# A hybrid sliding-window and sparse attention block: value products one head later, search passes dealt by new weights, indexer scores in groups of four, five key slots

## What is computed

```
A: q k^T / 8 - slope * |distance|, window of two 64-token chunks,
   softmax with a learned sink per head, times v        (8 heads, 2 key/value heads)
B: score[t, s] = sum over 4 indexer heads of w[t, h] * relu(q_idx[t, h] . k_idx[s])
   each query keeps the 256 keys of the highest score among those visible to it,
   ties broken by position; softmax over those, times v (8 heads, one shared key/value)
```

## Time and profile before

| | |
|---|---|
| median of 3 runs | 3556.61 us (3550.65 to 3558.83) |
| the profiled execution's own time | 3546.74 us |
| its span | 3545.0 us |
| PE busy | 3068.2 us, 87% of the span |
| DVE busy | 1700.3 us, 48% |
| ACT busy | 1585.2 us, 45% |
| `mixing` in the span | about 105 to 1812 us |

### The profile page before, as it was taken

The page is one execution under the profiler, slowest core; times in us unless marked ns, Lnnn a source line. Parts: engine busy times, 40 slices in busy tenths (PEclk is TensorE's granted clock), DMA queues, the critical chain, the costliest instruction groups (busy, mean ns, idle before and its releaser), DMA issues. The chain is left out here.

```text
span 3545.0 us, 43989 instructions
## 1 busy us (share of the span) xinstructions
PE 3068.2 (87%) x14889; PEld 2499.4 (71%) x14889; DVE 1700.3 (48%) x3080; ACT 1585.2 (45%) x3023; POOL 305.4 (9%) x990
## 2 busy tenths in 40 slices
PE   5788887777887787686889789999999999999997
PEld 2566666665666665666778678788887888788876
DVE  2154556566566765774445444324442444244422
ACT  1356666567656676676443222223222322232222
POOL 0012221111111111111001100000000000000000
PEclk8777878778887888778799999999999999999999
DMA  5011110000000000000035533334333433343323
GB/s 199 21 42 39 32 35 24 18 16 19 25 22 14 14 24 10 4 7 1 5 135 166 170 103 98 91 119 142 95 95 113 142 95 98 111 141 100 95 89 107
DMA packets 316082, 254.94 MB, mean 72 GB/s; under 512 B 9152, under 2 KB 271904, under 8 KB 315808
## 3 DMA queue, kind: packets, MB, share of 16 engines
q1 hardware_dynamic: 282544, 236.29, 21.5%
q10 hardware_dynamic: 33392, 16.81, 1.6%
HBM read 219.50 MB, written 33.57 MB: 71 GB/s over the span
## 5 line engine op out<-in xcount | busy, mean ns | idle before, releaser
L1928 ACT ACTIVATE p_hi<-raw 128x1024 fp32r<-128x1024 f32 x264 | 279.4, 1059 | 695.0 <-PE dbank L1899 356.1
L2002 DVE TENSOR_TENSOR p_lo<-raw,p_hi 128x1024 fp32r<-128x1024 f32 x264 | 323.5, 1225 | 426.9 <-ACT p_hi L1928 426.7
L826 PE MATMUL obank<-vb,probT 128*128 128x64 f32 x2176 | 344.7, 308 | 88.0 <-ACT probT L1084 87.6
L826 PEld LDWEIGHTS obank<-vb,probT 128*128 128x128 f32 x2176 | 333.9, 231 | 98.7 <-ACT probT L1084 98.5
L1084 ACT ACTIVATE probT<-tbank 128x512 f32<-128x512 f32 (+3 forms) x448 | 213.8, 487 | 347.1 <-PE tbank L810 342.8
L1108 ACT ACTIVATE relu<-score,pick 128x512 bf16<-128x512 f32 (+6 forms) x224 | 303.8, 1356 | 48.5 <-POOL pick L603 47.5
L1255 DVE TENSOR_SCALAR_CACHE_REDUCE above<-score,cand 128x384 bf16<-128x384 f32 (+6 forms) x224 | 316.0, 1411 | 4.8
L1880 PE MATMUL gbank<-x_hi,p_hi 128*128 128x512 f32 x704 | 275.5, 391 | 29.4 <-DVE p_lo L2002 29.4
L693 PE MATMUL work<-w_in,h_T 128*128 128x512 f32 (+1 forms) x768 | 298.0, 537 | 0.7 <-ACT h_T L892 0.7
L1897 PE MATMUL dbank<-p_hi,a_hi 128*128 128x512 f32 x704 | 279.0, 396 | 17.0 <-DVE a_lo L2030 14.1
L795 PE MATMUL lbank<-kb,qb_hi 128*128 128x512 f32 (+3 forms) x320 | 170.6, 533 | 138.0 <-DVE mx L1315 92.2
(11 more groups left out here) (219 smaller groups left out, 5314.4 us busy)
## 6 DMA issues: line engine op xcount, KB each, us to landing
raw<-in_w_gate_up SPq DMA_DIRECT2D x176, 512.0 KB, 3.8
raw<-in_w_down SPq DMA_DIRECT2D x88, 512.0 KB, 3.8
ada<-in_w_ada ACTq DMA_DIRECT2D x32, 512.0 KB, 3.8
wada<-in_w_ada SPq DMA_DIRECT2D x4, 2048.0 KB, 15.5
x_in<-in_x SPq DMA_DIRECT2D x16, 512.0 KB, 3.9
mixT<-oT SPq DMA_DIRECT2D x32, 256.0 KB, 2.3
mix<-mixT SPq DMA_DIRECT2D x16, 512.0 KB, 6.2
x_rows<-in_x SPq DMA_DIRECT2D x16, 512.0 KB, 4.4
```

What stands on the lines that cost most here:

```text
L826: mm = nc.tensor.matmul(obank[o % 2][:, h * HD:(h + 1) * HD], probT[:, t % 2, j * P:(j + 1) * P], v, start=(g == 0 and j == 0), stop=(last ...
L1928: nc.scalar.activation(p_hi[:, s], raw[:, s], ACT.Copy).then_inc(panel_high, 1)
L2002: nc.vector.tensor_tensor(p_lo[:, s], raw[:, s], p_hi[:, s].bitcast(F32), ALU.subtract).then_inc(panel_ready, 1)
```

## The change

- **Value products.** `copy_transposed` writes the transposed group back to the bytes of the `logit` row that it came from, and `probT` is gone. `logit` has four rows. All value products of head i-3 are now beside the pieces of head i and the transposes of head i-2; output scaling, turning and copying come a head later each. DVE's first piece of head i waits for `pv_done` of head i-4 in place of `pt_full` of head i-3.
- **Search passes.** `slot_weight` is replaced by one weight function for DVE and one for ACT. Both `ties` actions of a DVE-searched block are in its last slot. On ACT, when more than one sign pass is in a head, one each is put behind the first and the third copy of a transposed group.
- **Scores.** One step per piece of keys, four pairs of products each: the first where the burst was, the next ones after A heads 0, 1 and 2. The projection parts move one head later, the queries of B one head earlier (after A head 2).
- **Keys of A.** `ka` has five slots; a tile whose number is a multiple of four (but the first) is written to slots 0 and 4, so that two neighbouring tiles always lie side by side, and an A head has one pair of products over 256 columns in place of two pairs over 128.
- **Buffers.** `signs` is a tile of its own in int8 and no longer waits for the relus, `above` is uint8 in place of bf16, `bias_v` is gone (`bias_b` serves blocks 0 and 1), and the key/value latent has its own tile `latT_kv`.

```diff
@@ -187,8 +187,29 @@
     return b % 2 == 1
-def slot_weight(kind, b):
-    return 3.0 if kind == "A" else 2.5 + 0.45 * (b + 1)
+def vector_weight(b, slot):
+
+    it, kind, h = slot
+    scoring = it + 2 < NB and h <= 3
+    if kind == "A":
+        return (0.0 if it == b - 2 else 0.5) if scoring else 3.3
+    room = 0.5 + 0.41 * (it + 1)
+    if it + 3 < NB and h in (2, 4, 6):
+        room -= 1.0
+    if it == b - 2 and b > 2:
+        room -= {6: 2.0, 7: 100.0}.get(h, 0.0)
+    return max(room, 0.0)
+
+
+def scalar_weight(b, slot):
+
+    it, kind, h = slot
+    if kind == "A":
+        return 0.0 if it == b - 2 and h <= 3 else 1.8
+    room = 0.5 + 0.3 * (it + 1)
+    if it + 3 < NB:
+        room -= {1: 2.5, 3: 2.5, 5: 2.5, 6: 1.0}.get(h, 0.0)
+    return max(room, 0.3)
@@ -210,16 +231,16 @@
         slots += [(it, "B", h) for h in range(HEADS)]
     vector, scalar = {}, {}
     if searched_by_scalar(b):
-        wts = [slot_weight(kind, it) for it, kind, h in slots[:-2]]
+        wts = [scalar_weight(b, slot) for slot in slots[:-2]]
         for slot, r in zip(slots, spread(wts, len(ON_SCALAR))):
             scalar[slot] = [(b, ON_SCALAR[n]) for n in r]
         vector[slots[-2]] = [(b, AFTER_SCALAR[0])]
         vector[slots[-1]] = [(b, action) for action in AFTER_SCALAR[1:]]
     else:
-        wts = [0.0 if (it, kind, h) == (b - 2, "B", HEADS - 1) else slot_weight(kind, it) for it, kind, h in slots[:-1]]
-        for slot, r in zip(slots, spread(wts, len(SEARCH) - 1)):
+        wts = [vector_weight(b, slot) for slot in slots[:-1]]
+        for slot, r in zip(slots, spread(wts, len(SEARCH) - 2)):
             vector[slot] = [(b, SEARCH[n]) for n in r]
-        vector[slots[-1]] = [(b, SEARCH[-1])]
+        vector[slots[-1]] = [(b, action) for action in SEARCH[-2:]]
     return vector, scalar
@@ -257,8 +278,8 @@
     def front_a(b, h):
-        add(*{0: [("transposes", b)], 2: [("proj", b, 0)], 3: [("proj", b, 1)], 4: [("proj", b, 2)],
-              5: [("proj", b, 3)], 6: [("proj", b, 4)]}.get(h, []))
+        add(*{0: [("transposes", b)], 3: [("proj", b, 0)], 4: [("proj", b, 1)], 5: [("proj", b, 2)],
+              6: [("proj", b, 3)], 7: [("proj", b, 4)]}.get(h, []))
...
@@ -285,7 +306,9 @@
             steps.append(("head", "A", nxt, h, tuple(vector.get(at, ())), tuple(scalar.get(at, ()))))
             if b + 3 < NB:
                 front_a(b + 3, h)
-            if h == 3:
+            if h + 1 < len(key_chunks("B", nxt)):
+                add(("scores", nxt, h + 1))
+            if h == 2:
                 add(("queries", "B", b))
             if h in (1, 7):
@@ -347,6 +370,13 @@
     return [(o, min(BANK, cols - o)) for o in range(0, cols, BANK)]
+def key_slots(t):
+
+    if t == 0 or t % 4:
+        return t % 4, lambda ap: ap
+    return slice(0, 5, 4), lambda ap: ap.unsqueeze(2).to_broadcast([HD, A_KV, 2, P])
+
+
 class Plan:
...
@@ -406,10 +436,9 @@
         neg_half = sb("neg_half", [P, 1])
         ndist = sb("ndist", [P, T], F16)
         bias_a = sb("bias_a", [P, 2 * P])
-        bias_v = sb("bias_v", [P, 2 * P])
         bias_b = sb("bias_b", [P, T])
-        ka = sb("ka", [P, A_KV, 4, P], F32R)
+        ka = sb("ka", [P, A_KV, 5, P], F32R)
         ki = sb("ki", [P, T], F32R)
         kb = sb("kb", [P, T], F32R)
         va = sb("va", [P, 4, P])
@@ -425,13 +454,15 @@
         pj = sb("pj", [P, D_IN])
         kk = sb("kk", [P, 3, 2, HD])
         lat = sb("lat", [P, Q_RANK + KV_RANK])
-        latT = sb("latT", [P, 3, 3, P])
+        latT = sb("latT", [P, 3, 2, P])
+        latT_kv = sb("latT_kv", [P, P])
         widx = sb("widx", [P, 2, IDX_HEADS])
         ssq = sb("ssq", [P, 3])
...
         score = sb("score", [P, 2, T])
-        above = sb("above", [P, T], BF16)
+        above = sb("above", [P, T], mybir.dt.uint8)
+        signs = sb("signs", [P, T], mybir.dt.int8)
         rank = sb("rank", [P, T], F16)
         cand = sb("cand", [P, 1], I32)
...
-                    spans = [(j * P, P, ka[:, g, t % 4, :]) for j, t in enumerate(key_tiles(kind, b))]
+                    first = (b - 1) % 4 if b else 0
+                    spans = [(0, n, ka[:, g, first:first + n // P, :])]
...
-                    mm = nc.tensor.matmul(obank[o % 2][:, h * HD:(h + 1) * HD], probT[:, t % 2, j * P:(j + 1) * P], v,
+                    mm = nc.tensor.matmul(obank[o % 2][:, h * HD:(h + 1) * HD], 
+                                          logit[:, i % 4, (4 * g + j) * P:(4 * g + j + 1) * P], v,
                                           start=(g == 0 and j == 0), stop=(last and j == len(tiles) - 1))
@@ -844,17 +875,16 @@
                 n = len(plan.heads)
                 pieces = len(key_chunks(*plan.heads[i][0:2])) if i < n else 0
                 groups = len(plan.groups(i - 2)) if 2 <= i < n + 2 else 0
-                for c in range(max(pieces, groups, 1)):
+                values = len(plan.groups(i - 3)) if 3 <= i < n + 3 else 0
+                for c in range(max(pieces, groups, values)):
                     if c < pieces:
                         piece(i, c)
                     if c < groups:
                         transpose_group(i - 2, c)
-                    if c == 0 and 3 <= i < n + 3:
-                        weighted_values(i - 3, len(plan.groups(i - 3)) - 1)
-                    if 1 <= c < groups:
-                        weighted_values(i - 2, c - 1)
-                if i >= 4:
-                    turn_output(i - 4)
+                    if c < values:
+                        weighted_values(i - 3, c)
+                if 5 <= i < n + 5:
+                    turn_output(i - 5)
...
-                nc.scalar.activation(ka[0:HD, :, b % 4, :], pairs(keys[0:HD, 0:2 * P]), ACT.Copy)
+                slots, twice = key_slots(b)
+                nc.scalar.activation(ka[0:HD, :, slots, :], twice(pairs(keys[0:HD, 0:2 * P])), ACT.Copy)
...
-                copy_out(latT[:, b % 3, 2, :], ps[:, 3 * P:4 * P])
+                copy_out(latT_kv[:], ps[:, 3 * P:4 * P])
...
-            def copy_transposed(i, first):
-
-                for g, tiles in enumerate(plan.groups(i)):
-                    if (g < 2) != first:
-                        continue
-                    t = plan.group0[i] + g
-                    n = P * len(tiles)
-                    act.wait_ge(pt_full, t + 1)
-                    if t >= 2:
-
-                        act.wait_ge(pv_done, t - 1)
-                    nc.scalar.activation(probT[:, t % 2, 0:n], tbank[t % 2][:, 0:n], ACT.Copy).then_inc(pt_ready, 1)
+            def copy_transposed(i, g):
+
+                n = P * len(plan.groups(i)[g])
+                t = plan.group0[i] + g
+                act.wait_ge(pt_full, t + 1)
+                o = 4 * P * g
+                nc.scalar.activation(logit[:, i % 4, o:o + n], tbank[t % 2][:, 0:n], ACT.Copy).then_inc(pt_ready, 1)
             def copy_output(i):
...
-                act.wait_ge(relu_used, relus[0])
                 act.wait_ge(pick_ready, 34 * nth + j + 1)
                 nc.scalar.activation(signs[:, 0:L], score[:, b % 2, 0:L], ACT.Sign, scale=-1.0,
                                      bias=pick[:].bitcast(F32), accum_out=less_more[:]).then_inc(signs_summed, 1)
-                signs_made[0] = 32 * nth + j + 1
             def head(i, actions=()):
                 n = len(plan.heads)
-                if i >= 5:
-                    copy_output(i - 5)
-                if 2 <= i < n + 2:
-                    copy_transposed(i - 2, True)
-                if 1 <= i <= n:
-                    exponent(i - 1)
-                if 2 <= i < n + 2:
-                    copy_transposed(i - 2, False)
-                for b, action in actions:
-                    sum_signs(b, action)
+                groups = len(plan.groups(i - 2)) if 2 <= i < n + 2 else 0
+                waiting = list(actions)
+                if 6 <= i < n + 6:
+                    copy_output(i - 6)
+                for g in range(max(groups, 1)):
+                    if g < groups:
+                        copy_transposed(i - 2, g)
+                    if g in (0, 2) and len(waiting) > 1:
+                        sum_signs(*waiting.pop(0))
+                    if g == min(1, max(groups, 1) - 1) and 1 <= i <= n:
+                        exponent(i - 1)
+                for action in waiting:
+                    sum_signs(*action)
             act.wait_ge(weights_in, 16 * N_W)
...
-                if b > 2:
-
-                    dve.wait_ge(piece_read, plan.last_piece("B", b - 1))
+
+                dve.wait_ge(piece_read, plan.last_piece("B", b - 1))
@@ -1300,9 +1322,9 @@
                 pieces = len(key_chunks(kind, b))
                 o, n = key_chunks(kind, b)[c]
                 m = plan.chunk0[i] + c
-                if c == 0 and i >= 3:
-
-                    dve.wait_ge(pt_full, plan.group0[i - 2])
+                if c == 0 and i >= 4:
+
+                    dve.wait_ge(pv_done, plan.group0[i - 3])
```

(47 more changed lines are left out.)

74 lines of the change are left out of this document (38 added, 36 removed).

## The result

| | before | after |
|---|---|---|
| median | 3553.63 us (3547.46 to 3558.83, 4 runs) | 3510.09 us (3509.01 to 3513.44, 4 runs) |
| ratio | | 0.988 (0.9861 to 0.9899) |
| span of the profiled execution | 3545.0 us | 3511.7 us |
| PE busy | 3068.2 us | 3019.1 us |

Faster by 1.2%, where 3.8% was forecast (3422 us); the time lies inside the stated range (3290 to 3535), in the direction forecast, at a third of the size. It is 3 us from the rival "the wait only moves" (3507 us).

A forecast was written before the change was run, and what follows sets the result against it. PE, busy 87% of the span, was taken as the bound, with some 280 us of waits and half-clock time to win. Terms summed to -135 us: 3412 us profiled, 3422 us as median, range 3290 to 3535 us.

The forecast's parts named there:

- the wait only moves: Rival: ACT as late as before, PE waits at the transposes instead of the value products; median 3507 us, chance 0.22.
- term 4: Scores in groups: burst waits removed, smaller group waits added, products at better clock; -22 us, ends -78 and +110.
- Term 1: B heads: value products a head later give 1.8 us more cover against ACT's late copies; -52 us.
- Term 5: Search passes: dealing worth nothing, ACT passes between copies hide part of its wait for POOL; -10 us.
- Term 2: Both tie steps in the last slot: seven DVE waits for ACT's square, and PE's behind them, shrink; -36 us.
- Term 3: A heads: one product pair instead of two, two products fewer in each of 120 heads; -20 us.
- Terms 8 and 9: Gains given back as B heads meet DVE's own time, +23 us; a tail one head longer, +2 us.
- Term 6: PE's clock: fewer long waits, so less half-clock work after them; -28 us, ends 0 and -60.
- Term 7: DVE's addition with uint8 `above` mixes types and slows to 2.3 us for 2048 columns; +8 us.
- The rival of the groups: Each score group meets ACT behind a sign pass and PE stands 6 us; median 3593 us, chance 0.07.
- The rival of the clock: With PE's gaps short, the loop falls to 1.2 GHz less often; median 3346 us, chance 0.24.

The follow-up runs named there:

- x1: Changed kernel, but the first projection part waits only for ACT's two copies of the transposed input: 3427.83 us, ratio 0.9634.
- x13: Kernel of x10 with all of ACT's passes at the end of the head, value products late: 3510.03 us, ratio 0.9886.
- x12: Kernel of x10 with value products at their old place, ACT's passes still between the copies: 3470.50 us, ratio 0.977.
- x10: Of the change only late value products, buffers and types, tie steps in the last head, and ACT's passes between copies: 3476.93 us, ratio 0.978.
- x3: Changed kernel with the value products at their old place, copies still written into the row: 3516.49 us, ratio 0.989.
- x5: Kernel of x1 with the value products at their old place: 3436.89 us, ratio 0.9686.
- x7: Kernel of x1 with the old search-pass weights on both engines, none in a search's first four A heads: 3439.7 us, ratio 0.9688.
- x4: Kernel before, with only both tie steps of DVE-searched blocks put in the last head: 3544.83 us, ratio 0.9976.
- x6: Kernel of x1 with two product pairs of 128 columns per A head again: 3455.18 us, ratio 0.973.
- x2: Changed kernel with scores as one burst again, projection parts and queries at their old heads: 3438.31 us, ratio 0.9668.
- x8: Kernel of x1 with ACT's weight lowest in B head 7, so none holds two sign passes: 3401.86 us, ratio 0.9581.

## Why the prediction was wrong

- **The step that failed** is the last sentence of term 4: that the projection parts move with the scores, need the same time, and nothing follows from it but `gains`. The wait of part 0 on all earlier uses of the work banks was not read against the new order, nor that ACT takes the queries one head late. The term put it at nothing; it cost 82 us (x1). With that wait mended the kernel takes 3427.83 us, 6 us from the forecast.
- That closeness is partly luck, as the other terms were off in both directions. **Term 1** (-52): 34 us alone, between nothing and 9 beside the interleaving (x13, x12 against x10, x3, x5; 18 by the ratios of x5). It expected less than 40 us of new waiting at the transposes, which came (48.3 us against 10.9), but left out the score banks, whose wait is 19 us longer with late values (x3). **Term 5** (-10): the weights are worth 12 (x7), the interleaving alone 74 (x12). It was priced as a quarter of ACT's wait for POOL; the term left out that the copies that PE needs now pass between the passes. **Term 2** (-36): 8 to 11 us, given back at the scores (x4). **Term 3** (-20): 27 us (x6). **Term 4** (-22), without the accident: 10 us (x2 against x1). These single numbers add up to 131 to 143 us, near the 128 us between the kernel before and x1. Terms 8 and 9 were not tried apart.
- **Term 6** (clock, -28) had its mechanism right: products are slower behind a stall. Its size cannot be read apart from the stalls that it was tied to; where those at the value products went or shrank, PE's busy time fell by 18 to 25 us (x12, x13). What the term could not foresee is the stall that the change made, with 31.6 us of slower products in the rows of the changed kernel against x1.
- **Term 7** was exact in its row: the addition takes 2291 ns for 2048 columns. That agrees with the rule of the Trainium skill ("VectorE: DVE Perf Modes", section "What auto-detection actually checks"), by which the doubled rate needs every tensor to be 16-bit. (By the term's own figures it should have read +9, not +8.) What it costs in time was not tried apart. The row of the changed kernel, by forms:

```profile
L1313 DVE TENSOR_TENSOR above<-above,h_T 128x2048 uint8<-128x2048 uint8 x1 | 2.3, 2291 | 0.0
```

- **The rival "the wait only moves"** gave 3507 us and was 3 us off, but its claim holds only beside the interleaving; its number came out because 82 us of new wait stood against gains that it denied. **The rival of the groups** looked in the right place (an engine met behind a sign pass, the long chain of x8) at the wrong price: the groups' waits were 53.6 + 9.5 us in all. **The rival of the clock** (3346 us) did not come; its row gave 0.86 at the end of the loop, where it reckoned with 0.90, and the changed loop has 0.82.
- Of what was to be seen in the changed profile, the value products' wait, `negmax`, the 120 products and the 2.3 us addition came as written; the scores waited 67 us (53.6 + 9.5 + 4.0) instead of 57. The clock of the loop was 0.82, not above 0.84, the seven waits on the square fell only to 22.0 us in nine, and the score banks stayed at 116 us, near the 120 that was to speak against it.

## What to carry to other kernels

When a step moves in an order that all engines share, read every wait of that step as it stands in the code against the new order; one that says "all uses before mine" takes in whatever is moved ahead of it. If an engine that a chain needs has a row of long passes, try putting the chain's small steps between them: here that was worth 74 us. A longer pipeline was worth 34 us without it and nothing beside it, so price cures that act on one wait together, and try them in all four combinations. And move a step towards its last possible place only after looking at what is queued behind it there.

## What the runs showed of the hardware that was not expected

- A stall of PE can cost more than its length: eight 512-column products took 6.45 us behind a wait of 4.89 us, where the clock stood at 0.50, and 3.65 us in x1 without the wait, at 1.00. Over 13 such waits 58.4 us of waiting cost 82 us.
- DVE's multiply-add of two tensors over 512 columns (L1241) takes 0.75 us mostly, but 2.71 to 2.74 us when it runs beside POOL's addition to `x_in`. In the changed kernel this addition runs 16 times. Seven times no multiply-add overlaps it, and it takes 2.34 us; nine times one does, and it takes 2.47 to 2.54 us, while the multiply-add (384 columns once, 512 else) takes 2.60 to 2.74 us. So DVE pays some 2 us and POOL some 0.2. Two of the 16, one of each kind, and the multiply-add beside the second (shortest, median and longest in ns, then its start):

```profile
482.07 2.34 POOL L686 TENSOR_TENSOR x_in<-x_in,pre 128x1024 f32<-128x1024 f32 x1 [6.36 <-DVE x_in L1190]
...
575.26 2.52 POOL L686 TENSOR_TENSOR x_in<-x_in,pre 128x1024 f32<-128x1024 f32 x1 [7.82 <-DVE x_in L1190]
...
L1241 DVE SCALAR_TENSOR_TENSOR score<-relu,widx,score x1: 2712/2712/2712, 575.6 to 575.6; 128x512 f32<-128x512 f32 x1
```

  The Trainium skill ("SBUF — State Buffer", section "Who interferes with whom") says that a DVE instruction with two SBUF inputs contends with a GpSimd instruction that reads SBUF. The rows agree, with and without the overlap. In x8, 13 of the 16 additions meet a multiply-add.
